# Gate projections by seven products between the steps of attention, in a one-core hybrid decoder trunk

## Chip, cores and metric

One core of one Trainium2 chip runs the whole program. The metric is the device time of one execution in microseconds (us), weights read from HBM included. All numbers are float32. The engines are TensorE (PE in the rows; PEld is its weight load), VectorE (DVE), ScalarE (ACT), GpSimd (POOL) and SyncE (SP), which issues the loads.

## What is computed

Two layers over 256 tokens of width 1024. Each layer has a mixer, a cross attention and a mixture of experts. The change lies in the mixer, of which this is the core:

```python
proj = hn @ w_in                      # columns: z, xbc, dt, q, k, v, qi, ki, wi, g_ssd, g_attn
y_ssd = ssd_branch(z, xbc, dt_raw, ...)        # scan, y * silu(z), RMSNorm in 4 groups
y_attn = dsa_branch(q, k, v, qi, ki, wi)       # top-64 keys per query, softmax, values
merged = (jax.nn.sigmoid(g_ssd) * (y_ssd @ w_ssd_o)
          + jax.nn.sigmoid(g_attn) * (y_attn @ w_attn_o))
return merged @ w_out
```

The gates g_ssd and g_attn are 1024 columns of the projection each: the products of the normalised input with two times two chunks of 512 columns.

## The kernel before

`make_order` writes out one list of stages, ORDER. Every engine goes through it and issues its own part of each stage (`stage` in each engine's block), so an engine's order is the list's order, and waits between engines are semaphores. `make_jobs` makes from ORDER the list of jobs, a job being one filling of a PSUM bank; job k uses bank (k + SHIFT) mod 8, so TensorE may fill it only when job k-8 has been read ("drained") by its owner, VectorE or ScalarE.

Weights come in chunks of 512 columns into four slots of `wring`. SP loads a chunk when the last job of the chunk four before it is filled.

Most projections use a scheme of seven products (`seven`): input and weights are cut in quarters, and seven products of quarters and of sums of quarters replace eight. PRODUCTS gives their order, 1, 2, 5, 6, 3, 7, 4. VectorE makes the sums of the input's quarters once (`sums`), four sums of weight quarters for each chunk (`weight_sums`, numbers 1 to 4), and from the seven products the four quarters of the result. ScalarE copies products 1 and 5 out of their banks (`products_1_and_5`). For the chunks of z the work is spread over the steps of the SSD scan: TensorE computes in a stage `("part", ("z", n), half)` products 1, 2, 5, 6 or 3, 7, 4, and VectorE's work on them (`join`) stands one step later. `combine` is the same work for chunks done in one piece.

The gates are done by `by_channel`: half a chunk is 16 matmuls of 256 columns, which the trace shows as 32 instructions, into two halves of a bank, and ScalarE writes their sigmoid to `gateT`.

Attention runs in six pairs of jobs. Step m of ORDER holds, in this order: the softmax division of pair m-1 (`soft`: a reciprocal and a product on VectorE), the scores of pair m (`score`: TensorE; then on VectorE the sum with the mask, the maximum and its scaling; then on ScalarE the exponentials), half a gate chunk (`part`), for m below 4 the products of y and silu(z) (`ygate`: VectorE, then squares on ScalarE), at m = 4 the normalisation of y (`ynorm`: VectorE, POOL's power, eight scalings on VectorE), the transposes of the probabilities of pair m-1 (`probT`, copied by VectorE), the product with the values of pair m-2 (`pv`, copied by ScalarE), and from m = 5 on the transposes of y (`yT`, copied by VectorE and ScalarE in turn). There are eight such steps, m = 0 to 7; steps 6 and 7 have no scores. Behind them stand `("sums", "y")` and the output projection of the SSD branch (`ssdo`), which needs all of yT.

The lines of the rows below: L785 is a matmul of `by_channel`, L816 one of `seven` with 128 columns, L819 one with 256, L742 a transpose, L960 a score, L980 a `pv`, L1475 a sum of weight quarters, L1492, L1495, L1504 and L1630 the sums of a join, L1722 to L1731 VectorE's part of an `ssd` stage, L1737 `ygate`, L1745 `ynorm`, L1760 to L1764 VectorE's part of a score, L1776 and L1778 `soft`, L1784 the copy of `probT`, L1287 a gate's sigmoid, L1347 a score's exponential, L1328 an exponential over 1024 columns in the SSD scan, L1268 a copy of yT.

## Time and profile before

| what | us |
|---|---|
| median of 3 runs | 1552.94 (1552.15 to 1553.21) |
| the profiled execution | 1552.55 |
| its span | 1550.4 |
| TensorE busy | 1407.3 |
| VectorE busy | 811.8 |
| ScalarE busy | 369.0 |

The span is what the profile covers of the execution; 2.15 us lie around it. The mean granted clock of TensorE is 0.971. Layer 0 runs to about 777 us and layer 1 from there; the attention steps lie from 234 to 313 us and from 1002 to 1081 us, the expert phases from about 555 to 777 and from about 1320 on. A row of the timeline gives the start, the time from the start of the first to the end of the last instruction, the engine, the line and how many instructions it merges; behind it, in brackets, how long the engine was idle before it and who ended that.

### The profile page before, as it was taken

Reading aid. Unit: us, or ns where it says so; the run is one execution under the profiler, and the core shown is the slowest. Engines: PE = TensorE matmul, PEld = TensorE weight load, DVE = VectorE, ACT = ScalarE, POOL = GpSimd, SP = SyncE. Lnnn points to the kernel's source line nnn. Section 1 sums busy time; section 2 is a strip of 40 time slices with the busy share of each in tenths; the row PEclk is TensorE's granted clock in tenths of the full one; section 3 lists DMA queues with packets and bytes.
Section 4 is the critical chain, followed back from the end, with each engine's and each line's share of the span. In section 5 each row is a group of like instructions: output and inputs, shape, how many; then the busy total and the mean of one; then the engine's idle time right before and its main releaser. Section 6 shows DMA issues by size and latency. Waiting matters only on the chain. (4 is left out here: it accounts for less than half of the span.)

```text
span 1550.4 us, 23297 instructions
## 1 busy us (share of the span) xinstructions
PE 1407.3 (91%) x9428; PEld 1098.2 (71%) x9428; DVE 811.8 (52%) x1562; ACT 369.0 (24%) x830; POOL 74.9 (5%) x64
## 2 busy tenths in 40 slices
PE   7999999999999978767699999999999999787684
PEld 5888888899998544334278888888999985444241
DVE  3488877577974332212135888765679643321122
ACT  2222457301111121001122234573021021110010
POOL 0000520000000000000000015100000000000000
PEclk9999999999999998899999999999999999998898
DMA  8434223246441689999963443333374408899996
GB/s 301 162 137 148 99 108 110 109 145 251 180 163 55 271 343 381 419 416 417 392 224 119 154 163 109 109 109 110 112 291 161 167 7 335 367 381 416 416 418 256
DMA packets 115706, 350.06 MB, mean 226 GB/s; under 512 B 11664, under 2 KB 13968, under 8 KB 99216
## 3 DMA queue, kind: packets, MB, share of 16 engines
q1 hardware_dynamic: 114912, 345.95, 58.1%
q0 software_dynamic: 688, 2.62, 0.4%
q8 instruction: 76, 1.25, 0.3%
q14 instruction: 30, 0.25, 0.0%
HBM read 347.50 MB, written 1.05 MB: 225 GB/s over the span
## 5 line engine op out<-in xcount | busy, mean ns | idle before, releaser
L785 PE MATMUL bank<-hT,wring 128*128 128x256 f32 x1280 | 281.9, 380 | 0.0
L785 PEld LDWEIGHTS bank<-hT,wring 128*128 128x128 f32 x1280 | 241.3, 190 | 35.9 <-issue 3.3
L1128 PE MATMUL bank<-wring,big 128*32 128x256 f32 x2048 | 140.8, 436 | 60.7 <-DMA wring<-in_w_up_e 44.4
L1128 PEld LDWEIGHTS bank<-wring,big 128*32 128x32 f32 x2048 | 70.9, 125 | 128.6 <-DMA wring<-in_w_up_e 48.2
L2033 DVE TENSOR_TENSOR h<-bank,h 128x512 f32<-128x512 f32 x64 | 44.3, 692 | 111.4 <-PE bank L1171 111.4
L2026 DVE TENSOR_TENSOR big<-bank,big 128x256 f32<-128x256 f32 x16 | 6.8, 425 | 167.4 <-ACT big L1395 167.4
L1099 PE MATMUL bank<-big,xn 128*128 128x256 f32 x256 | 74.5, 453 | 14.8 <-DVE big L1951 14.8
L1644 DVE SCALAR_TENSOR_TENSOR scr<-bank,prm,scr 128x255 f32<-128x255 f32 (+1 forms) x144 | 62.7, 477 | 47.4 <-ACT scr L1236 44.7
L1099 PEld LDWEIGHTS bank<-big,xn 128*128 128x128 f32 x256 | 67.2, 335 | 24.4 <-DVE big L1951 19.7
L816 PE MATMUL bank<-big,wring 128*128 128x128 f32 x704 | 81.3, 275 | 2.3 <-ACT big L1268 2.0
L816 PEld LDWEIGHTS bank<-big,wring 128*128 128x128 f32 x704 | 80.0, 192 | 3.0 <-issue 2.9
L1201 ACT ACTIVATE ga<-bank 128x256 f32<-128x256 f32 x48 | 18.4, 383 | 261.2 <-PE bank L816 186.1
L819 PE MATMUL bank<-wring,hT 128*128 128x256 f32 x288 | 66.1, 379 | 0.0
L819 PE MATMUL bank<-wring,xn 128*128 128x256 f32 x288 | 65.1, 379 | 0.0
L1171 PE MATMUL bank<-big 128*128 128x512 f32 x128 | 62.2, 618 | 0.1
L819 PEld LDWEIGHTS bank<-wring,xn 128*128 128x128 f32 x288 | 54.5, 190 | 10.9 <-issue 2.6
L819 PEld LDWEIGHTS bank<-wring,hT 128*128 128x128 f32 x288 | 54.4, 190 | 9.8 <-issue 2.9
L1395 ACT ACTIVATE big<-bank 128x256 f32<-128x256 f32 x16 | 6.1, 384 | 229.2 <-PE bank L1128 229.2
L766 PE MATMUL bank<-wring,qq 128*128 128x512 f32 x128 | 56.6, 595 | 0.0
L686 POOL TENSOR_TENSOR sums<-sums,cst 128x2 f32<-128x2 f32 (+2 forms) x11 | 9.0, 819 | 911.3 <-DVE sums L1428 661.2
L1475 DVE TENSOR_TENSOR wring<-wring 128x1024 f32<-128x1024 f32 (+1 forms) x36 | 51.5, 1430 | 1.2
L816 PE MATMUL bank<-hT,wring 128*128 128x128 f32 x448 | 51.7, 275 | 0.0
(320 smaller groups left out, 2228.1 us busy)
## 6 DMA issues: line engine op xcount, KB each, us to landing
wring<-in_w_in SPq DMA_DIRECT2D x68, 1024.0 KB, 7.0
wring<-in_w_gate_e SPq DMA_DIRECT2D x16, 4096.0 KB, 20.3
wring<-in_w_up_e SPq DMA_DIRECT2D x16, 4096.0 KB, 21.2
wring<-in_w_ssd_o SPq DMA_DIRECT2D x16, 1024.0 KB, 6.2
wring<-in_w_ckv SPq DMA_DIRECT2D x16, 1024.0 KB, 7.4
scr<-in_w_down_e SPq DMA_DIRECT2D x8, 2048.0 KB, 28.1
ga<-in_w_down_e SPq DMA_DIRECT2D x8, 2048.0 KB, 30.3
qq<-in_w_down_e SPq DMA_DIRECT2D x8, 2048.0 KB, 25.8
```

Of the source, the lines that this page charges most:

```text
L686: nc.gpsimd.tensor_tensor(r, r, cst[:, C_MH:C_MH + r.shape[1]], ALU.pow).then_inc(rstd_rdy, 1)
L766: ins = nc.tensor.matmul(bank[bank_of(job)][:, 0:width], src[:, k, t * P:(t + 1) * P], wring[:, SLOT[c], k, 0:width], start=i == 0, stop=i ...
L785: ins = nc.tensor.matmul(bank[bank_of(job)][:, i * SEQ:(i + 1) * SEQ], wring[:, SLOT[c], k, m:m + P], src[:, k, :], start=n == 0, stop=n = ...
L816: ins = nc.tensor.matmul(b[:, i * P:(i + 1) * P], w[:, j, i * P:(i + 1) * P], x[:, j, :], start=j == 0, stop=j == k - 1)
L819: ins = nc.tensor.matmul(b[:, 0:HALF_W], x[:, j, :], w[:, j, :], start=j == 0, stop=j == k - 1)
L1099: return nc.tensor.matmul(bank[banks[c // 2]][:, (c % 2) * E * S:(c % 2 + 1) * E * S], xn_eighth[:, k, c, :], sel[:, k, :], start=start, s ...
L1128: ins = nc.tensor.matmul(bank[b][j * S:(j + 1) * S, i * F:(i + 1) * F], xg[:, k, e:e + S], up_part[i][:, j, k * F:(k + 1) * F], start=k == ...
L1171: nc.tensor.matmul(bank[6 + n][:, :], selT[:, b, k * P:(k + 1) * P], yg[:, n * NCOL:(n + 1) * NCOL], start=True, stop=True).then_inc(sct_s, 1)
L1201: drain_inc(nc.scalar.activation(to, bank[bank_of(JOB[(st, p)])][:, 0:HALF_W], ACT.Copy), JOB[(st, p)])
L1475: V.tensor_tensor(out, a, b, ALU.subtract).then_inc(wsum_rdy, 1)
L1644: ins = V.scalar_tensor_tensor(conv[:, m % 2, i, k:SEQ], b[:, i * SEQ:(i + 1) * SEQ - k], prm[:, w:w + 1], conv[:, m % 2, i, k:SEQ], ALU.m ...
L2033: V.tensor_tensor(hh, bank[6 + n][:, :], hh, ALU.add).then_inc(add_s, 1)
```

## The change

It does five things in each layer:

- the four gate chunks are made by seven products, four of them in the first half and three in the second; their joins stand a step later, between `soft` and `score`;
- the chunks come in the order attention gate, then SSD gate (`GATES`);
- the sigmoid is taken of a whole gate at a time, in `gateT` in place: of the attention gate in step 5, ahead of score 5, of the SSD gate behind the last join;
- the copies of `probT` and all copies of yT go to ScalarE, and the eight scalings of `ynorm` too;
- the router's weights, whose place in `btok` now holds temporaries of the joins, are loaded later.

```diff
@@ -80,6 +80,9 @@
 PAIRS = [(t, i) for t in range(2) for i in range(2 * (t + 1))]
 ATT = [(t, r, i) for t, i in PAIRS for r in range(2)]
 SSD = [(t, g) for t in range(TT) for g in range(SG)]
+
+
+GATES = [("gate", 1, 0), ("gate", 1, 1), ("gate", 0, 0), ("gate", 0, 1)]
 
 
 def make_order():
@@ -102,9 +105,13 @@
     for m in range(len(PAIRS) + 2):
         if 1 <= m <= len(PAIRS):
             o += [("soft", 2 * m - 2), ("soft", 2 * m - 1)]
+        if m:
+            o += [("join", GATES[(m - 1) // 2], (m - 1) % 2)]
+        if m == 5:
+            o += [("sigmoid", 1)]
         if m < len(PAIRS):
             o += [("score", m)]
-        o += [("part", ("gate", m // 4, m // 2 % 2), m % 2)]
+        o += [("part", GATES[m // 2], m % 2)]
         if m < 4:
             o += [("ygate", 2 * m), ("ygate", 2 * m + 1)]
         if m == 4:
@@ -115,6 +122,7 @@
             o += [("pv", m - 2)]
         if m >= 5:
             o += [("yT", i) for i in ((0, 1), (2, 3, 4), (5, 6, 7))[m - 5]]
+    o += [("join", GATES[3], 1), ("sigmoid", 0)]
     o += [("sums", "y"), ("ssdo", 0), ("ssdo", 1), ("sums", "att"), ("atto", 0), ("mem",), ("atto", 1), ("sums", "merged")]
     o += [("memT", i) for i in range(4)] + [("sums", "mem"), ("wo", 0), ("wo", 1)]
     o += [("norm", 1), ("ck", 0)] + [("hT", 1, i) for i in range(4)] + [("ck", 1), ("sums", "h")]
@@ -145,8 +153,8 @@
     "hT": (1, "both"), "small": (2, "dve"), "kv": (2, "dve"), "qi": (2, "dve"), "xbc": (2, "dve"),
     "acum": (1, "dve"), "kT": (1, "dve"), "kiT": (1, "dve"), "qiT": (1, "act"), "idx": (2, "act"),
     "xT": (1, "act"), "bT": (1, "act"), "cb": (1, "dve"), "qT": (1, "act"), "decay": (2, "act"),
-    "score": (2, "dve"), "probT": (1, "dve"), "pv": (1, "act"), "gate": (2, "act"),
-    "yT": (1, "both"), "memT": (1, "act"),
+    "score": (2, "dve"), "probT": (1, "act"), "pv": (1, "act"),
+    "yT": (1, "act"), "memT": (1, "act"),
     "xscore": (1, "act"), "xprobT": (1, "act"), "xpv": (1, "dve"), "co": (2, "dve"),
     "hX": (1, "act"), "router": (1, "dve"), "rank": (1, "dve"), "count": (1, "dve"),
 }
@@ -158,10 +166,10 @@
     return ["dve", "act" if SSD[n][0] == 0 else "dve"]
 
 
-SEVEN = {"q": "h0", "z": "h0", "ssdo": "y", "atto": "att", "wo": "merged", "ck": "mem", "cv": "mem", "cq": "h"}
+SEVEN = {"q": "h0", "z": "h0", "gate": "h0", "ssdo": "y", "atto": "att", "wo": "merged", "ck": "mem", "cv": "mem", "cq": "h"}
 PRODUCTS = (1, 2, 5, 6, 3, 7, 4)
 HALVES = (PRODUCTS[:4], PRODUCTS[4:])
-EARLY = ("q", "z")
+EARLY = ("q", "z", "gate")
 UNITS = [st[1] if st[0] == "part" else st for st in ORDER
          if st[0] in SEVEN or st[0] == "part" and st[1][0] in SEVEN and st[2] == 0]
 FIRST_OF = {"h0": (("q", 0), (1, 2)), "y": (("ssdo", 0), (1, 2, 3))}
@@ -377,6 +385,7 @@
         *late_temps, whole0, whole1 = [cols(att, i * HALF_W, HALF_W) for i in range(7)]
         wholes = [whole0, whole1]
         early_temps = [cols(mix, 1792 + i * HALF_W, HALF_W) for i in range(3)] + [cols(att, 1536 + i * HALF_W, HALF_W) for i in range(2)]
+        gate_temps = early_temps[:3] + [cols(btok, i * HALF_W, HALF_W) for i in range(2)]
         sums_of = {"h0": xn[:, :, :].rearrange("p t (s k n) -> p (t s) k n", s=2, n=P),
                    "y": [cols(big, 4096 + i * 1024, KC, P) for i in range(2)]
                    + [cols(hT[:, :, :].rearrange("p c t -> p (c t)"), i * 1024, KC, P) for i in range(2)],
@@ -404,10 +413,14 @@
 
         def temps(st):
 
+            if st[0] == "gate":
+                return gate_temps
             return early_temps if st[0] in EARLY else late_temps
 
         def spare_sums(st):
 
+            if st[0:2] == ("gate", 0):
+                return cols(scr, 2048, KC // 2, HALF_W), cols(scr, 3072, KC // 2, HALF_W)
             if st[0] in EARLY:
                 return cols(ga, 0, KC // 2, HALF_W), cols(ga, 1024, KC // 2, HALF_W)
             if st[0] == "ssdo":
@@ -477,6 +490,7 @@
         wsum_rdy = sem("sums_of_weight_quarters")
         q_rdy = sem("queries_roped")
         z_rdy = sem("z_silu_ready")
+        g_rdy = sem("gate_sigmoid_ready")
         mem_sq = sem("mem_squares")
         mem_eps = sem("mem_mean_square")
         mem_rstd = sem("mem_rstd_ready")
@@ -652,9 +666,9 @@
                         settle(sp)
                         src = w_down[l, 1, 0:BE].rearrange("j (k p) n -> p k j n", p=P)
                         sp.dma_start(mix_rows, src[:, 0]).then_inc(mix_in, 16)
-                    if c == CHUNK[(("ssdo", 1), 1)]:
-
-                        filled(sp, l, JOB[(("ssd", SG - 1), 1)])
+                    if c == CHUNK[(("cq", 0), 0)]:
+
+                        drained(sp, l, JOB[(GATES[3], 4)])
                         settle(sp)
                         sp.dma_start(rw[:, :, 0:G], rows(w_group[l], 0, G)).then_inc(router_in, 16)
                         sp.dma_start(rw[:, :, G:G + G * E], rows(w_router[l], 0, G * E)).then_inc(router_in, 16)
@@ -833,14 +847,12 @@
                 elif kind in ("small", "kv", "qi"):
                     by_token(l, st, hT, {"small": SH + HD + IH, "kv": 2 * AKV * HD}.get(kind, NCOL),
                              blocks_by={k: JOB[(("hT", 0, k // 2), 0)] for k in range(KC)} if kind == "small" else None)
-                elif kind == "part" and st[1][0] == "gate":
-                    by_channel(l, st[1], hT, tiles=st[2:3])
                 elif kind == "part" and st[1][0] == "co":
                     by_token(l, st[1], qT, tile_by=CO_TILE_BY, tiles=st[2:3], ks=range(KC // 2 if st[2] else 0, KC))
                 elif kind == "open":
                     by_token(l, st[1], qT, tile_by=CO_TILE_BY, tiles=st[2:3], ks=range(KC // 2))
                 elif kind == "part":
-                    seven(l, st[1], {}, products=HALVES[st[2]])
+                    seven(l, st[1], {}, by_channel=st[1][0] == "gate", products=HALVES[st[2]])
                 elif kind == "q":
                     seven(l, st, {})
                 elif kind == "xbc":
@@ -1279,13 +1291,28 @@
                         if n >= 2:
                             act.wait_ge(rel_used, l * 2 * len(IDX) + (n - 1))
                         drain_inc(nc.scalar.activation(rel[:, n % 2, :], bank[bank_of(job)][:, :], ACT.Relu), job)
-                elif kind == "part" and st[1][0] == "gate":
-                    _, st, j = st
-                    job = JOB[(st, j)]
+                elif kind == "sigmoid":
+
+                    g = st[1]
+                    drained(act, l, JOB[(("gate", g, 1), 4)])
+                    for i in range(2):
+                        rows = gateT[g][:, 4 * i:4 * i + 4, :].rearrange("p c t -> p (c t)")
+                        ins = nc.scalar.activation(rows, rows, ACT.Sigmoid)
+                    ins.then_inc(g_rdy, 1)
+                elif kind == "ynorm":
+
+                    act.wait_ge(rstd_rdy, l * NORMS + 2)
+                    for t in range(TT):
+                        for g in range(SG):
+                            y = xs[:, t, g * NCOL:(g + 1) * NCOL]
+                            ins = nc.scalar.activation(y, y, ACT.Copy, scale=st_[:, 8 + t * SG + g:9 + t * SG + g])
+                    ins.then_inc(yn_rdy, 1)
+                elif kind == "probT":
+                    n = st[1]
                     filled(act, l, job)
-                    blk = 4 * st[2] + 2 * j
-                    drain_inc(nc.scalar.activation(gateT[st[1]][:, blk:blk + 2, :].rearrange("p c t -> p (c t)"),
-                                                   bank[bank_of(job)][:, :], ACT.Sigmoid), job)
+                    if n >= 4:
+                        filled(act, l, JOB[(("pv", (n - 4) // 2), 0)])
+                    drain_inc(nc.scalar.activation(pT[:, n % 4, :], bank[bank_of(job)][:, :], ACT.Copy), job)
                 elif kind == "part" and st[1][0] in SEVEN:
                     if st[2] == 0:
                         products_1_and_5(l, st[1])
@@ -1626,6 +1653,10 @@
 
                     def put(a, b, x, y, op):
 
+                        if of[0] == "gate":
+                            blk = 4 * of[2] + 2 * b
+                            dst = gateT[of[1]][:, blk:blk + 2, a * P:(a + 1) * P]
+                            return V.tensor_tensor(dst, x.rearrange("p (c t) -> p c t", t=P), y.rearrange("p (c t) -> p c t", t=P), op)
                         n = of[1] * NCOL + b * HALF_W
                         return V.tensor_tensor(zt[:, a, n:n + HALF_W], x, y, op)
 
@@ -1738,12 +1769,7 @@
                 elif kind == "ynorm":
 
                     dve.wait_ge(ssq_rdy, (l + 1) * len(SSD))
-                    rms(l * NORMS + 2, st_[:, 0:8], st_[:, 8:16], NCOL)
-                    for t in range(TT):
-                        for g in range(SG):
-                            y = xs[:, t, g * NCOL:(g + 1) * NCOL]
-                            ins = V.tensor_scalar(y, y, st_[:, 8 + t * SG + g:9 + t * SG + g], None, ALU.mult)
-                    ins.then_inc(yn_rdy, 1)
+                    V.tensor_scalar(st_[:, 8:16], st_[:, 0:8], 1.0 / NCOL, EPS, ALU.mult, ALU.add).then_inc(var_rdy, 1)
                 elif kind == "score":
                     for r in range(2):
                         n = 2 * st[1] + r
@@ -1776,12 +1802,6 @@
                     link(V.reciprocal(rs[:, n % 4, 0:nh], sm[:, n % 4, 0:nh]))
                     s3 = sco[:, n % 4, :].rearrange("p (h s) -> p h s", h=nh)
                     V.tensor_tensor(s3, s3, bc(rs[:, n % 4, 0:nh], 2, NCOL // nh), ALU.mult).then_inc(pr_rdy, 1)
-                elif kind == "probT":
-                    n = st[1]
-                    filled(dve, l, job)
-                    if n >= 4:
-                        filled(dve, l, JOB[(("pv", (n - 4) // 2), 0)])
-                    drain_inc(V.tensor_copy(pT[:, n % 4, :], b), job)
                 elif kind == "xpv":
                     t, pr = divmod(st[1], 2)
                     filled(dve, l, job)
@@ -1794,7 +1814,7 @@
 
                         blk = 4 * st[1] + 2 * b
                         rows, ts = slice(blk, blk + 2), slice(a * P, (a + 1) * P)
-                        drained(dve, l, JOB[(("gate", g, st[1]), b)])
+                        dve.wait_ge(g_rdy, l * 2 + 2 - g)
                         whole = wholes[(a + b) % 2]
                         link(V.tensor_tensor(whole, x, y, op))
                         of = whole.rearrange("p (c t) -> p c t", t=P)
```

What moves is told by the order of the built programs. The first place is VectorE in an odd and an even step (rows print the line of their own kernel; `bank` is PSUM, `scr` at that place is `gateT`, `ga` holds scores, `mix` and `btok` the temporaries). Before, from the gatings of y in step 3 to the scores of step 4:

```order
L1737 TENSOR_TENSOR xs<-xs,big 128x512 [waits z_silu_ready] x2
L1784 COPY qq<-bank 128x512 [waits bank_filled] x2
L1776 RECIPROCAL rs<-sm 128x2 [waits score_exp_ready]
L1778 TENSOR_TENSOR ga<-ga,rs 128x512 [waits dve_step]
L1776 RECIPROCAL rs<-sm 128x2 [waits score_exp_ready]
L1778 TENSOR_TENSOR ga<-ga,rs 128x512 [waits dve_step]
L1760 TENSOR_TENSOR ga<-bank,mix 128x512 [waits bank_filled]
```

With the change:

```order
L1768 TENSOR_TENSOR xs<-xs,big 128x512 [waits z_silu_ready] x2
L1802 RECIPROCAL rs<-sm 128x2 [waits score_exp_ready]
L1804 TENSOR_TENSOR ga<-ga,rs 128x512 [waits dve_step]
L1802 RECIPROCAL rs<-sm 128x2 [waits score_exp_ready]
L1804 TENSOR_TENSOR ga<-ga,rs 128x512 [waits dve_step]
L1659 TENSOR_TENSOR scr<-bank,btok 128x2x128 [waits bank_filled]
L1502 TENSOR_TENSOR scr<-wring 128x1024 [waits bank_filled,chunk_in2]
L1502 TENSOR_TENSOR scr<-wring,scr 128x1024 [waits bank_filled,sums_of_weight_quarters]
L1531 TENSOR_TENSOR btok<-bank,mix 128x256 [waits bank_filled]
L1659 TENSOR_TENSOR scr<-btok,mix 128x2x128 [waits drained_by_dve]
L1659 TENSOR_TENSOR scr<-btok,bank 128x2x128 [waits bank_filled,dve_step]
L1786 TENSOR_TENSOR ga<-bank,mix 128x512 [waits bank_filled]
```

The copies of `probT` have gone, and six sums, two of them over 1024 columns, stand between the divisions and the next score. The second place is ScalarE behind the exponentials of step 4. Before:

```order
L1287 ACT_TABLE_LOAD
L1287 ACTIVATE scr<-bank 128x512 [waits bank_filled]
L1368 ACTIVATE qq<-bank 128x2x128 [waits bank_filled]
L1347 ACT_TABLE_LOAD
L1347 ACTIVATE ga,sm<-ga,nmx 128x256 [waits score_max_ready]
```

With the change:

```order
L1213 ACTIVATE mix<-bank 128x256 [waits drained_by_dve,bank_filled] x2
L1308 ACTIVATE xs<-xs,sums 128x512 [waits rstd_ready]
L1308 ACTIVATE xs<-xs,sums 128x512 x7
L1315 ACTIVATE qq<-bank 128x512 [waits bank_filled] x2
L1395 ACTIVATE qq<-bank 128x2x128 [waits bank_filled]
L1300 ACT_TABLE_LOAD
L1300 ACTIVATE scr<-scr 128x1024 [waits drained_by_dve]
L1300 ACTIVATE scr<-scr 128x1024
L1374 ACT_TABLE_LOAD
L1374 ACTIVATE ga,sm<-ga,nmx 128x256 [waits score_max_ready]
```

The scalings of y, the copies of `probT` and the sigmoid of a whole gate now stand between the exponentials of step 4 and those of step 5; in the other steps the pairs of table loads are gone.

## Rows read from the trace of the kernel before

**Rows 1.** Busy time by stretch: layer 0's attention, one step of it, the expert phase.

```profile
core 0: us, PE busy (x) PEld busy (x) DVE busy (x) ACT busy (x) POOL busy (x), PEclk, DMA share, GB/s
234.02:313.26 79.24, 78.22 (x442) 64.05 (x441) 47.56 (x100) 45.82 (x114) 1.65 (x1) 1.00 0.30 110
251.29:261.34 10.05, 10.05 (x53) 7.82 (x53) 7.97 (x17) 7.55 (x19) 0.00 (x0) 1.00 0.59 210
560.00:790.00 230.00, 170.47 (x1458) 89.61 (x1448) 45.10 (x100) 29.31 (x57) 0.70 (x1) 0.91 0.98 397
```

**Rows 2.** Timeline of TensorE, one step of attention in layer 1.

```profile
1030.27 7.17 PE L785 MATMUL bank<-hT,wring 128*128 128x256 f32 x32
1037.28 1.04 PE L742 MATMUL bank<-cst,ga 128*128 128x128 f32 x8
1038.25 1.08 PE L980 MATMUL bank<-qq,mix 128*64 128x512 f32 x4
1039.26 1.13 PE L960 MATMUL bank<-mix,qq 64*128 64x256 f32 x8
```

**Rows 3.** Timeline of TensorE, products of the SSD output projection, layer 1.

```profile
1088.35 7.31 PE L816 MATMUL bank<-big,xs 128*128 128x128 f32 x64
1095.50 7.31 PE L816 MATMUL bank<-hT,wring 128*128 128x128 f32 x64
```

**Rows 4.** Timeline of VectorE, soft and score of step 5, layer 1.

```profile
1050.29 0.15 DVE L1776 RECIPROCAL rs<-sm 128x2 f32<-128x2 f32 x1
...
1051.89 0.68 DVE L1760 TENSOR_TENSOR ga<-bank,mix 128x512 f32<-128x512 f32 x1
...
1053.53 0.69 DVE L1760 TENSOR_TENSOR ga<-bank,mix 128x512 f32<-128x512 f32 x1
```

**Rows 5.** Groups by line and shape, VectorE, 234 to 313 us.

```profile
L1784 DVE COPY qq<-bank 128x512 f32<-128x512 f32 x12 | 7.7, 686 | 15.4 <-PE bank L742 15.4
...
L1737 DVE TENSOR_TENSOR xs<-xs,big 128x512 f32<-128x512 f32 x8 | 5.1, 684 | 0.0
```

**Rows 6.** Timeline of VectorE, the scalings of y, layer 0.

```profile
278.05 3.26 DVE L1745 TENSOR_SCALAR xs<-xs,sums 128x512 f32<-128x512 f32 x8 [1.76 <-POOL sums L686]
```

**Rows 7.** Timeline of VectorE, joins of z, layer 0.

```profile
210.72 0.41 DVE L1630 TENSOR_TENSOR big<-bank,ga 128x256 f32<-128x256 f32 x1
...
214.96 0.69 DVE L1722 TENSOR_TENSOR xs<-bank,xs 128x512 f32<-128x512 f32 x1 [0.19 <-PE bank L935]
...
219.42 1.21 DVE L1475 TENSOR_TENSOR wring<-wring 128x1024 f32<-128x1024 f32 x1
220.56 0.41 DVE L1630 TENSOR_TENSOR big<-bank,mix 128x256 f32<-128x256 f32 x1
...
230.62 0.42 DVE L1630 TENSOR_TENSOR big<-bank,ga 128x256 f32<-128x256 f32 x1
```

**Rows 8.** Timeline of ScalarE, second score of step 2, layer 0.

```profile
257.19 0.51 ACT L1347 ACTIVATE ga<-ga,nmx 128x256 f32<-128x256 f32 x1 [0.55 <-DVE nmx L1764]
...
258.30 1.28 ACT L1287 ACT_TABLE_LOAD   x1
259.59 0.60 ACT L1287 ACTIVATE ga<-bank 128x512 f32<-128x512 f32 x1
```

**Rows 9.** Groups by line and shape, ScalarE, whole program.

```profile
L1328 ACT ACTIVATE scr<-scr 128x1024 f32<-128x1024 f32 x16 | 16.9, 1057 | 0.4
```

**Rows 10.** Timeline of ScalarE, a copy of yT, layer 0.

```profile
302.45 0.84 ACT L1268 ACTIVATE big<-bank,prm 128x256 f32<-128x256 f32 x2 [0.63 <-PE bank L742]
```

**Rows 11.** Queue of SP around the loads of router weights and of w_cq, layer 0.

```profile
311.38 2.87 SPq L660 DMA_DIRECT2D btok<-in_w_router  x1
...
427.04 15.17 SPq L593 DMA_DIRECT2D wring<-in_w_cq  x4
```

**Rows 12.** Start of layer 1: busy time by stretch, and TensorE's timeline.

```profile
775.00:780.00 5.00, 2.66 (x13) 2.69 (x14) 1.80 (x4) 1.77 (x3) 0.70 (x1) 0.72 1.05 390
...
777.34 3.50 PE L742 MATMUL bank<-cst,xn 128*128 128x128 f32 x16 [5.30 <-ACT xn L1211]
```

## The prediction

> **What bounds the kernel now.** I read four views, from coarse to fine. Busy time by stretch comes first. In the expert phase TensorE has 0.74 of the time and the DMA engines 0.98 [rows 1]: weights arrive as fast as they can, so that phase neither hides a change ahead of it nor gives time back; it starts later or earlier by as much as the phase before it ends. In the attention steps TensorE is busy for the whole of a step (10.05 of 10.05 us), VectorE for 7.97 and ScalarE for 7.55, at a granted clock of 1.00 [rows 1]. The timeline of such a step says what the 10.05 us are: 7.01 for half a gate chunk, 0.97 for the eight transposes of probabilities, 1.01 for the product with the values, and the rest, 1.06, for the scores [rows 2]. So TensorE's own work is the bound in all eight steps, and VectorE sits beside it with about 2 us to spare in a step. The stretch from the first score (234.02 us) to the first product of the SSD output projection (313.26) lasts 79.2 us [rows 1] and stands in both layers.
>
> **The change, part by part, for one layer.** A step m runs from score m to score m+1. I hand results from VectorE or ScalarE on with 0.2 us (the waits of 0.19 in [rows 7] are of that size) and from TensorE with 0.33, a choice with which the same laying-out gives back the measured stretch.
>
> *TensorE, removed and added.* Eight half chunks of 7.01 us go: 56.1. A product of two quarters is 16 instructions with 128 columns; four such products start 7.15 us apart [rows 3]. Four half chunks of four products (7.15) and four of three (5.36) are 50.0 us. If nothing else moved, a layer would gain 6.1 us.
>
> *VectorE, removed.* Twelve copies of transposed probabilities, 0.686 us each, 8.2 in all, and four pairs of scalings of yT [rows 5]; and the eight scalings of y, 3.26, with the wait for POOL's power ahead of them, 1.76 [rows 6]. All of it lay in VectorE's spare time.
>
> *VectorE, added.* The first half of a join is two sums of weights and three of products: 1.14 (start to start) + 1.22 + three sums at 0.41, with their hand-overs 1.28, = 3.64 us. The second half, with the first two weight sums of the next chunk in it, is 4.05 (4.24 between its start and the next operation's, of which 0.19 is that one's own wait) [rows 7]. These are joins of z; those of the gates have the same shapes. The join of z that stands last before attention starts at 230.62 and gets two weight sums more; at 4.06 it ends at 234.7. The three operations of the last SSD part, 0.69 each and 2.35 with hand-overs, follow, and the first score's own work begins at 237.0. What stays on VectorE: two softmax divisions 1.62, two scores 2 x 1.64 = 3.28 [rows 4], in steps 0 to 3 two gatings of y 1.26 (0.68 each, 0.63 start to start) [rows 5].
>
> *The steps, VectorE against TensorE.* VectorE needs 1.62 + 3.64 + 3.28 + 1.26 = 9.80 us for an odd step and 1.62 + 4.05 + 3.28 + 1.26 = 10.2 for an even one; TensorE needs 1.06 + 5.36 + 0.97 + 1.01 = 8.40 and 1.06 + 7.15 + 0.97 + 1.01 = 10.19. A pair is 20.0 us on VectorE and 18.6 on TensorE; before, it was 20.1. TensorE can't run ahead, since a product's bank comes free only with the join of the step before, and that join stands behind the softmax of its own step. So VectorE becomes the bound up to step 4, and the saving is eaten there. I laid the steps one behind the other from 237.0: VectorE ends its scores of steps 1 to 4 at 251.4, 261.6, 271.4 and 280.6. In an even step TensorE gets its first bank only at the join's first operation and its second 2.8 us later, behind the two weight sums; so it finishes step 4 at 283.8 (now 281.4) though it has less to do.
>
> *ScalarE, steps 4 and 5.* Here is the one long wait that I expect. ScalarE has finished the exponentials of step 4 at 281.7, copies two products (0.76), scales y eight times at 0.52 (4.2; nearest row: a copy of 512 columns, 0.60 long and 0.49 to the next), copies two probT and one pv (1.4): 288.2. Then it loads the sigmoid's table, 1.28, runs two sigmoids over 1024 columns, near 2.1 by an exponential of that size, loads the exponential's table, 1.28 [rows 8, 9], and only then, at 292.8, takes the exponentials of step 5, whose maxima were ready at 289.7. They take 1.1 a score, the first ends at 293.9, both divisions at 296.0; VectorE was idle for 4.4 us. Its first sum of the next join then frees the bank for gate part 6. TensorE, done with step 5 at 293.1, starts it at 296.5, its second product at 299.3, behind two weight sums, and has finished the part at 304.7.
>
> *The end.* From there TensorE is the bound again: transposes, pv and three yT 3.3, gate part 7 5.4, pv 1.0; the first of the last three yT is filled at 314.9. All three are now copied by ScalarE, 0.84 each [rows 10], behind a pv copy: 317.8. The SSD projection starts at 317.95. The same laying-out with the kernel before gives 313.40 for a measured 313.26, so the method is good to some tenths there. The difference is 4.6 us a layer. Behind it the last sigmoid (1.28 + 2.1) lies beside the projection's first 7 us and is hidden; without that cover it would cost 3.4. The loads of router weights (issue 2.87 us) go from behind the last load of w_ssd_o to between two loads of w_cq, whose four issues now span 15.17 us [rows 11]: they fill a gap of SP's queue and cost nothing; without the gap up to 2.9 us.
>
> *Table loads.* In the trace a load takes 1.28 us and the next ACTIVATE begins right behind it (258.30, 259.59 [rows 8]). The twelve loads in a layer's steps lay beside TensorE's work and their going gains nothing; two of the four left lie on the path above, at 1.28. The Trainium skill, page "ScalarE: Activation LUTs", section "What ACT_TABLE_LOAD costs", has some 1283 ns for the load and 1380 ns of drain with it for each switch. By that page the detour would be 2.8 us longer a layer and the time some 1567 us; the row shows no such drain, and the sum goes by the row.
>
> **The sum.** 2 x 4.6 = 9.2 us on the profiled execution's 1552.55: 1561.8, so 1562. The median of the runs, 1552.94, is 0.4 above that execution, which I leave in the rounding. Bounds: if only TensorE's work counted, 1552.6 - 12.2 = 1540.3; if hand-overs between engines cost 0.4 instead of 0.2, the same laying-out gives 6.0 us a layer, 1564.6.
>
> **Rivals.**
> *Faster: TensorE stays the bound.* The mechanism is bank reuse that costs nothing, because joins find their place while TensorE works. For it: VectorE is busy for 47.6 us of the stretch now [rows 1]; less 8.2, 3.3 and 3.5 for what goes (four pairs of yT at 0.84 to 0.88), and with 28.4 for the joins (4 x 3.64 + 3 x 4.05 + 1.66 for the last, which has no weight sums), that is some 61 us of the 73 that TensorE would need. Against it: each even step asks 10.2 us of VectorE in a fixed order. It decides if softmax and join of one step take under 8.4 us with the scores. Time: 1540.3. Chance 0.06.
> *No change: the detour of ScalarE is hidden.* If the exponentials of step 5 don't wait for the sigmoid and the two loads, VectorE's 4.4 us go, step 6 starts 4 us earlier, and 0.6 us a layer is left: 1553.7. Against it: the sigmoid of the first gate stands ahead of score 5 on ScalarE in the order shown. Chance 0.10.
> *Slower still: the clock falls.* TensorE would wait 3.4 us before gate part 6. Behind a wait of 5.30 us at a layer's start the granted clock was 0.72 over 5 us, which mixes 1.2 and 2.4 GHz, and 16 transposes took 3.50 us, where eight take 0.97 [rows 12, 2]. So a fall would cost near 1.6 us a layer: 1565. The Trainium skill, page "TensorE: Matmul & The Clock Gate", part 1, says that an idle array goes to 1.2 GHz and that activity gives 2.4 back; the fall in this row agrees; whether a wait of 3.4 us brings it, no row here shows. Chance 0.12, as the other waits before this point are under 2 us.
> *The forecast itself.* Chance 0.72, by itself 1557 to 1565.
>
> **Numbers.** 0.2% is 3.1 us, about what a measurement of this kernel can tell from no change. Slower by more than that: the forecast but for a small part, and the clock: 0.82. Within: 0.11. Faster: 0.07. The range goes from 1553, which takes in the hidden detour, to 1567, with the clock's fall and slower hand-overs; outside are the rival of 1540 and the tails, under 2 in 10.
>
> **What would show it.** Right: the first product of the SSD projection starts 4 to 5 us later than now from the layer's first score on, in both layers; waits of TensorE on VectorE near 1 to 2 us in steps 2 to 4 and one of 3 us or more at gate part 6; VectorE idle some 4 us for ScalarE's exponentials in step 5, behind two table loads and eight scalings; the stretches after it as long as before. Wrong: steps 1 to 4 shorter than 10 us on the mean, or VectorE waiting for banks that TensorE fills, or a difference that appears outside the two stretches of attention.

## The result, and the profile after

The changed kernel takes 1561.12 us (median of 6 runs, 1560.21 to 1563.34), the kernel before 1553.53 (6 runs, 1552.15 to 1554.97): ratio 1.0052, 95% interval 1.0042 to 1.0062. That is 7.6 us slower, against 9.2 in the forecast, and 0.9 below the forecast time of 1562.0. The profiled execution took 1560.21 us and its span is 1558.4, 8.0 above the span before.

Where the time went is read first from one window, from the first score to the first product of the SSD output projection (columns as in [rows 1]):

```profile
core 0: us, PE busy (x) PEld busy (x) DVE busy (x) ACT busy (x) POOL busy (x), PEclk, DMA share, GB/s
234.27:317.88 83.61, 75.73 (x634) 67.95 (x633) 61.97 (x117) 48.85 (x138) 1.65 (x1) 0.98 0.30 108
```

The stretch lasts 83.61 us and lasted 79.24 [rows 1]. TensorE is busy for 2.5 us less in it, VectorE for 14.4 more, ScalarE for 3.0 more, and the granted clock is no longer 1.00. In layer 1 it is 83.60 for 79.24. Behind it little moved: from the projection's first product to the first matmul whose operands are `wring` and `big`, in this order, with 256 columns, 127.79 us passed in layer 0 before and after. Further on, the router of layer 0 took 0.36 us longer, since TensorE waited 1.17 us for VectorE there and not 0.81; in layer 1 it did not. Why stays open.

Timeline of TensorE, changed kernel, layer 0: the scores of steps 2, 3 and 5, and every row of the stretch in which TensorE waited for another engine.

```profile
250.23 1.13 PE L972 MATMUL bank<-mix,qq 64*128 64x256 f32 x8
...
256.13 3.84 PE L830 MATMUL bank<-xn,ga 128*128 128x128 f32 x32 [0.67 <-DVE btok L1531]
...
261.80 1.13 PE L972 MATMUL bank<-mix,qq 64*128 64x256 f32 x8
264.58 3.84 PE L830 MATMUL bank<-xn,wring 128*128 128x128 f32 x32 [1.65 <-DVE scr L1659]
...
275.76 2.05 PE L830 MATMUL bank<-hT,wring 128*128 128x128 f32 x16 [0.61 <-DVE btok L1531]
...
283.20 1.13 PE L972 MATMUL bank<-mix,qq 64*128 64x256 f32 x8
...
296.07 5.44 PE L830 MATMUL bank<-hT,wring 128*128 128x128 f32 x32 [3.27 <-DVE ga L1659]
301.35 3.74 PE L830 MATMUL bank<-xn,scr 128*128 128x128 f32 x32
...
317.88 2.36 PE L830 MATMUL bank<-big,wring 128*128 128x128 f32 x19 [1.61 <-ACT big L1280]
```

Three waits on VectorE's joins in steps 2 to 4 (0.67, 1.65, 0.61) take the place of TensorE's solid steps [rows 2]; the score of step 5, at 281.45 before, starts at 283.20. Then comes the long one, 3.27 us, before gate part 6, and the first two products of that part need 5.28 us (296.07 to 301.35) where the next two need 3.57. The 1.61 at the end, for the last copy of yT, was 1.02 before.

That VectorE sets the pace up to step 4 is seen in its own busy time, the fourth column:

```profile
237.00:280.00 43.00, 40.00 (x338) 35.89 (x337) 40.55 (x79) 22.35 (x82) 0.00 (x0) 1.00 0.30 113
```

It is busy for 40.55 of 43.00 us, and its timeline shows no wait for another engine from 229.73 to 281.05; what is missing lies in the short hand-overs between its own operations.

Behind the long wait stands ScalarE. Its timeline, from the last exponential of step 4 to the first of step 5:

```profile
280.43 0.49 ACT L1374 ACTIVATE ga<-ga,nmx 128x256 f32<-128x256 f32 x1
280.83 0.19 ACT L1374 ACTIVATION_READ_ACCUMULATOR ga<-ga,nmx 128x1 f32 x1
280.92 0.63 ACT L1213 ACTIVATE mix<-bank 128x256 f32<-128x256 f32 x2
281.73 5.01 ACT L1308 ACTIVATE xs<-xs,sums 128x512 f32<-128x512 f32 x8 [0.17 <-POOL sums L700]
286.64 1.06 ACT L1315 ACTIVATE qq<-bank 128x512 f32<-128x512 f32 x2
287.60 0.37 ACT L1395 ACTIVATE qq<-bank 128x256 f32<-128x256 f32 x1
287.98 1.28 ACT L1300 ACT_TABLE_LOAD   x1
289.28 2.00 ACT L1300 ACTIVATE scr<-scr 128x1024 f32<-128x1024 f32 x2
291.30 1.28 ACT L1374 ACT_TABLE_LOAD   x1
292.60 0.51 ACT L1374 ACTIVATE ga<-ga,nmx 128x256 f32<-128x256 f32 x1
```

And VectorE, which has the maxima ready and waits for these exponentials before the divisions and the next join:

```profile
279.72 0.17 DVE L1790 TENSOR_SCALAR nmx<-mx 128x2 f32<-128x2 f32 x1
...
288.57 0.17 DVE L1790 TENSOR_SCALAR nmx<-mx 128x2 f32<-128x2 f32 x1
293.72 0.17 DVE L1802 RECIPROCAL rs<-sm 128x2 f32<-128x2 f32 x1 [4.98 <-ACT ga L1374]
...
295.51 0.42 DVE L1659 TENSOR_TENSOR ga<-bank,btok 128x256 f32<-128x256 f32 x1
```

The row at 295.51 is the join's first sum: it frees the bank for which TensorE waits until 296.07. What TensorE's clock did there is in windows of 2 us:

```profile
294.00:296.00 2.00, 0.00 (x0) 0.00 (x0) 1.88 (x5) 2.00 (x8) 0.00 (x0) 1.00 1.03 396
296.00:298.00 2.00, 1.93 (x12) 1.96 (x13) 1.97 (x2) 1.36 (x4) 0.00 (x0) 0.70 0.52 193
298.00:300.00 2.00, 2.00 (x11) 2.00 (x11) 1.93 (x5) 0.38 (x1) 0.00 (x0) 0.50 0.02 4
300.00:302.00 2.00, 2.00 (x19) 2.00 (x18) 1.13 (x2) 0.00 (x0) 0.00 (x0) 0.95 0.00 0
```

A granted clock of 0.50 is the lower level, 1.2 GHz: after the wait TensorE ran at half speed for most of two products.

### The profile page after: what moved, and what is told of

It reads as the page before. It is cut to its first block, busy times and chain, and to the rows that moved or that the text cites. A ratio compares the mean times of both kernels' runs of the same rounds, so it can differ in the third digit from the quotient of the medians.

```text
span 1558.4 us, 24237 instructions
## 1 busy us (share of the span) xinstructions
PE 1402.7 (90%) x9812; PEld 1106.3 (71%) x9812; DVE 842.4 (54%) x1594; ACT 378.0 (24%) x878; POOL 74.9 (5%) x64
## 4 chain that ended last, share of the span: by engine, by line
PE 66%; issue 16%; DMA 8%; DVE 6%; ACT 3%; SPq 0%; DVEq 0%; POOL 0%; POOLq 0%; ACTq 0%
PE bank L830 19%; PE bank L833 15%; PE bank L799 11%; PE bank L780 7%; DMA ga<-in_w_down_e 6%; PE bank L756 3%; PE bank L1111 2%; PE bank L1140 2%; PE bank L947 1%; DMA wring<-in_w_up_e 1%; PE bank L1183 1%; PE bank L1036 1%; PE bank L936 1%; DVE ga L1502 1%; PE bank L1166 1%
## 5 line engine op out<-in xcount | busy, mean ns | idle before, releaser
L799 PE MATMUL bank<-hT,wring 128*128 128x256 f32 x768 | 167.5, 380 | 0.0
L830 PE MATMUL bank<-hT,wring 128*128 128x128 f32 x832 | 102.2, 282 | 7.9 <-DVE ga L1659 6.5
L1502 DVE TENSOR_TENSOR wring<-wring 128x1024 f32<-128x1024 f32 (+1 forms) x44 | 61.2, 1392 | 1.2
```

The lines of the kernel that those rows point to most:

```text
L799: ins = nc.tensor.matmul(bank[bank_of(job)][:, i * SEQ:(i + 1) * SEQ], wring[:, SLOT[c], k, m:m + P], src[:, k, :], start=n == 0, stop=n = ...
L830: ins = nc.tensor.matmul(b[:, i * P:(i + 1) * P], w[:, j, i * P:(i + 1) * P], x[:, j, :], start=j == 0, stop=j == k - 1)
L1502: V.tensor_tensor(out, a, b, ALU.subtract).then_inc(wsum_rdy, 1)
```

## The experiments

The theory: up to step 5 VectorE sets the pace, because the joins and the sums of weights are on it; from step 5 on it is ScalarE's detour (scalings, table load, sigmoid, table load) and the clock behind the wait that it makes. Rivals: the moves to ScalarE are the cause by themselves; table loads drain the engine and cost more than their rows; the clock's fall has nothing to do with the wait.

Single profiled executions of these kernels differ by up to 3 us outside attention, on the way through the router and the experts of a layer. The stretch of attention does not: before, changed and the experiments repeat it between the layers to 0.02 us, but for two runs named below. So I judge by the stretch, split at the score of step 5, as read from TensorE's timeline (layer 0):

| kernel | score 0 to score 5 | score 5 to SSD projection | stretch | time, us |
|---|---|---|---|---|
| before | 47.43 | 31.81 | 79.24 | 1553.53 |
| changed | 48.93 | 34.68 | 83.61 | 1561.12 |
| e1 sigmoid at end | 48.93 | 29.54 | 78.47 | 1553.02 |
| e2 and sums behind join | 48.05 | 29.61 | 77.66 | 1551.20 |
| e3 more work on VectorE | 53.25 | 35.85 | 89.10 | 1572.45 |
| e4 narrow sums | 45.04 | 31.21 | 76.25 | 1546.62 |
| e5 scalings on VectorE | 48.93 | 36.23 | 85.16 | 1564.43 |
| e6 and sigmoid at end | 48.92 | 36.19 | 85.11 | 1564.05 |
| e7 moves alone | 47.42 | 32.40 | 79.82 | 1553.68 |
| e8 TensorE kept busy | 48.93 | 33.93 | 82.86 | 1560.86 |
| e9 Exp for Sigmoid | 48.94 | 31.07 | 80.01 | not readable |
| e10 e4 and e1 together | 45.04 | 29.54 | 74.58 | 1545.56 |

**e1: the sigmoid of step 5 goes behind the last join.**

```diff
-        if m == 5:
-            o += [("sigmoid", 1)]
...
-    o += [("join", GATES[3], 1), ("sigmoid", 0)]
+    o += [("join", GATES[3], 1), ("sigmoid", 1), ("sigmoid", 0)]
```

> The sigmoid of the attention gate goes from ahead of score 5 to behind the last join, beside the other one. Theory (ScalarE's detour holds the chain in step 5): VectorE no longer waits 5 us for the exponentials of step 5, TensorE's wait of 3.3 us before gate part 6 goes, and with it the fall of the clock; the stretch from the first score to the first product of the SSD projection goes from 83.6 to about 79.1 us in each layer, the time from 1561.1 to about 1552. Rival (VectorE's load alone is the cause): the wait moves elsewhere and the time stays within 1.5 us of 1561.

Measured: 1553.02 us (11 runs), ratio 0.9996, interval 0.9987 to 1.0005; stretch 78.47. All of the change's loss is gone, and in the stretch 0.8 us a layer besides. The time doesn't show that 0.8: the kernel before took 1553.44 us (21 runs) beside these runs. Timeline of TensorE at gate part 6, where the wait of 3.27 stood:

```profile
292.60 1.10 PE L754 MATMUL bank<-cst,xs 128*128 128x128 f32 x8
293.53 3.74 PE L828 MATMUL bank<-hT,wring 128*128 128x128 f32 x32
```

No wait, and two products in 3.6 us. The first five steps are the same to 0.01 us, so the sigmoid's place acts on what follows step 5 alone: 5.14 us. ScalarE still scales y for 5 us there; it is the first load, the sigmoids and the second load on top of that which made it late.

**e2: as e1, and the gates' first two sums of weights of the next chunk at the end of the join instead of in its middle.**

```diff
-                if after[0] in EARLY:
+                if after[0] in ("q", "z"):
                     weight_sums(l, after, (1, 2))
...
                 drain_inc(put(1, 0, part3, b, ALU.subtract), job)
+                if after[0] == "gate":
+                    weight_sums(l, after, (1, 2))
```

> As e1, and the first two weight sums of the next gate chunk stand at the end of a join's second half, no longer between its first and second operation, so that the banks of products 3, 7 and 4 come free earlier. Theory (in even steps TensorE waits for banks, 0.6 to 0.7 us each before product 2): stretch about 78.1 us, time about 1550, which is below the kernel before. Rival: product 5 then waits for the sums instead by as much, and the time equals that of e1.

Measured: 1551.20 us (11 runs), ratio 0.9988, interval 0.9979 to 0.9997; stretch 77.66. The banks come free before the 2.4 us of sums of weights instead of after them, and the first five steps are 0.9 us shorter. This is the one version that leaves nothing out and whose interval lies below the kernel before, by 0.12%, near the limit of what the runs can tell.

**e3: twelve reductions over 512 columns more on VectorE in each layer, one with each probT.**

```diff
+                elif kind == "probT":
+                    link(V.tensor_reduce(top8[:, 0:1], cst[:, 0:NCOL], AX_X, ALU.max))
```

> VectorE gets back, as a plain maximum over 512 columns of constants whose result nobody uses, the twelve operations of 0.69 us a layer that the change took from it (the copies themselves stay on ScalarE). Theory (VectorE is the bound of steps 1 to 4): about 3.7 to 5.5 us a layer longer, 1569 to 1572. Rival (VectorE has slack in these steps, the loss is all in step 5): within 1.5 us of 1561.

Measured: one execution, 1572.45 us; stretch 89.10, so of the 8.4 us added (1.40 a pair) 5.5 appear. Three of the six pairs stand ahead of the join of step 4, and that join and score 5 come 4.32 us later, which is all that these pairs take: VectorE has no slack there. Of the later pairs 2.3 us go into its wait for the exponentials, which falls from 4.98 to 2.70. The other 1.2 us of loss, behind score 5, match a longer fall of the clock. Two rows behind waits are

```profile
267.23 5.47 PE L830 MATMUL bank<-xn,wring 128*128 128x128 f32 x32 [3.09 <-DVE scr L1659]
...
300.16 6.62 PE L830 MATMUL bank<-hT,wring 128*128 128x128 f32 x32 [3.01 <-DVE ga L1659]
```

against 3.84 and 3.74 for such rows at full clock. From the start of the second row to that of the next product it is 6.46 us, for 5.28 in the changed kernel. The slow row at 267.23 costs nothing, for VectorE does not wait for its products.

**e4: the gates' sums of weights cut to one column (which leaves these sums out).**

```diff
+                    if st[0] == "gate":
+                        out, a, b = [v[:, 0:1, 0:1] for v in (out, a, b)]
                     V.tensor_tensor(out, a, b, ALU.subtract).then_inc(wsum_rdy, 1)
```

> The sixteen sums of weight quarters for the gates in each layer are cut to one column each; they signal as before. It leaves out nearly all of these sums, so the gates are not what they should be. Theory (VectorE's joins hold the bank reuse): steps 1 to 4 become TensorE's 8.4 to 10.2 us and the stretch goes to about 76 us in each layer, the time to about 1546, with the wait for ScalarE in step 5 still there. Rival (products wait for something else): over 1557.

Measured: one execution, 1546.62 us; stretch 76.25. The first five steps take 45.04 us for 48.93: 3.9 us a layer are what VectorE's sums of weights put on the path before score 5. VectorE's wait for the exponentials of step 5 is still there:

```profile
DVE rs L1804 <- ACT ga L1374: 4.4, 2, 4.2
```

That row of the waits (total, times, longest) has 4.2 us for the longest.

**e5 and e6: the eight scalings of y back on VectorE; e5 with the sigmoid in its place, e6 with both sigmoids at the end.**

```diff
-                            ins = nc.scalar.activation(y, y, ACT.Copy, scale=st_[:, 8 + t * SG + g:9 + t * SG + g])
...
+                            ins = V.tensor_scalar(y, y, st_[:, 8 + t * SG + g:9 + t * SG + g], None, ALU.mult)
```

> The changed kernel with the eight scalings of y back on VectorE, sigmoid in its place. Theory (the sigmoids hold the exponentials of step 5, and VectorE is short of time by about as much): VectorE gets 8 x 0.40 = 3.2 us more work in step 4 while ScalarE gets 5.0 us less; the exponentials come earlier, VectorE comes later, so nearly nothing is gained: stretch 83.3 us (changed kernel 83.6), time about 1560.5, and the wait of VectorE for the exponentials shrinks from 5.0 to under 2 us. Rival (the scalings in ScalarE's queue are the cause by themselves): 5.0 us of ScalarE's path go, up to the whole loss comes back: stretch about 79, time about 1552.

> The same with both sigmoids behind the last join, as in e1 (stretch 78.5 there, scalings on ScalarE). Theory: with the detour gone VectorE is what bounds, so its 3.2 us of scalings come onto the path and more by the hand-overs behind them: stretch 83.3 us, time about 1561, 4.8 us a layer over e1. Rival (ScalarE is the scarce engine, VectorE hides the scalings in its waits): as e1 or below it, 78.5 us, time 1553.

Measured, one execution each: 1564.43 and 1564.05 us, both slower than the changed kernel and than either expectation; stretches 85.16 and 85.11 in layer 0, but 83.71 and 83.64 in layer 1. The rivals fall: the scalings on ScalarE are not the cause, and taking them back is worth less than nothing. With them on VectorE the sigmoid's place changes nothing, since VectorE is the later of the two (its longest wait for exponentials is 0.4 us in both, for 4.98); with them on ScalarE it changes 5.1. The two layers of e5 differ at one place, gate part 5 (first row layer 0, second layer 1):

```profile
288.63 6.70 PE L830 MATMUL bank<-xn,wring 128*128 128x128 f32 x32 [3.76 <-DVE ga L1651]
...
1063.05 5.26 PE L830 MATMUL bank<-xn,wring 128*128 128x128 f32 x32 [3.77 <-DVE ga L1651]
```

The same wait, and 1.44 us between the rows, as between the stretches (1.45). The granted clock was 0.58 over the 8 us from 288 and 0.74 over the 6 us from 1063:

```profile
288.00:296.00 8.00, 7.37 (x40) 7.38 (x41) 7.13 (x16) 3.03 (x9) 0.00 (x0) 0.58 0.01 3
...
1063.00:1069.00 6.00, 5.95 (x40) 5.95 (x41) 5.54 (x11) 2.01 (x8) 0.00 (x0) 0.74 0.00 0
```

Against a row of 3.84 at full clock the fall cost 2.9 us in one layer and 1.4 in the other, and without it both stretches would be 82.3. My expectation of 83.3 had no term for a fall there. What made it longer in layer 0 stays open.

**e7: the kernel before with only the moves to ScalarE (copies of probT and yT, scalings of y).**

```diff
-    "score": (2, "dve"), "probT": (1, "dve"), "pv": (1, "act"), "gate": (2, "act"),
-    "yT": (1, "both"), "memT": (1, "act"),
+    "score": (2, "dve"), "probT": (1, "act"), "pv": (1, "act"), "gate": (2, "act"),
+    "yT": (1, "act"), "memT": (1, "act"),
...
```

The part left out moves the code of these copies and scalings to ScalarE, as in the change.

> The kernel before (gates as plain products, a sigmoid with each copy) with only the change's moves to ScalarE: copies of probT and of yT, scalings of y. Theory: TensorE bounds the steps there at 10.05 us and nothing else is late, so VectorE's relief is worth nothing until the tail, where the last three copies of yT stand on one engine instead of two: stretch 79.2 + 0.6 = 79.8 us, time about 1554.7 (ratio 1.0008). Rival (the moves by themselves cost what the change lost): 83.6 us, 1562. Rival (they gain, and the seven products cost more than was measured): below 78.5 us, under 1552.

Measured: 1553.68 us (10 runs), ratio 1.0004, interval 0.9994 to 1.0013; stretch 79.82, so 0.58 a layer, all of it behind score 5. The moves neither cost what the change lost nor gain.

**e8: the second yT job's four transposes issued seven times over, so that TensorE works through most of the wait.**

```diff
-                    ins = nc.tensor.transpose(b[:, i * P:(i + 1) * P], src, ident)
+                    ins = nc.tensor.transpose(b[:, i % 4 * P:(i % 4 + 1) * P], src, ident)
...
-                    transposes(l, JOB[(st, 0)], pairs(xs, st[1]))
+                    transposes(l, JOB[(st, 0)], pairs(xs, st[1]) * (7 if st[1] == 1 else 1))
```

> The changed kernel with the four transposes of the second yT job issued seven times over (28 in place of 4), so that TensorE is busy through most of the 3.3 us in which it waited at 293 to 296 us. Same results. Theory (the granted clock fell to 0.50 to 0.70 at 296 to 300 us because TensorE had stood still before): clock 1.00 there, first two products of part 6 take 3.6 us and not 5.3, but the second waits for its bank until 298.9, so the stretch is shorter by about 0.7 us a layer: 82.9 us, time about 1559.8. Rival (the fall has nothing to do with the wait): clock 0.5 to 0.7 in the same place, stretch 83.6 or longer, time 1561 or above.

Measured: 1560.86 us (4 runs; ratio to the kernel before 1.0053, interval 1.0037 to 1.0070); stretch 82.86. Timeline of TensorE and its clock at the place of the fall:

```profile
291.77 3.71 PE L756 MATMUL bank<-cst,xs 128*128 128x128 f32 x32
296.14 2.02 PE L830 MATMUL bank<-hT,wring 128*128 128x128 f32 x16 [0.66 <-DVE ga L1659]
298.78 2.05 PE L830 MATMUL bank<-hT,wring 128*128 128x128 f32 x16 [0.61 <-DVE btok L1531]
300.66 3.74 PE L830 MATMUL bank<-xn,scr 128*128 128x128 f32 x32
```

```profile
296.00:298.00 2.00, 1.86 (x16) 1.86 (x16) 1.97 (x2) 1.42 (x4) 0.00 (x0) 1.00 0.59 218
298.00:300.00 2.00, 1.39 (x13) 1.23 (x12) 1.93 (x5) 0.38 (x1) 0.00 (x0) 1.00 0.05 12
```

With work in place of the wait the clock stayed at 1.00, part 6 started no earlier, and its first two products took 4.52 us instead of 5.28: the fall cost 0.76. At full clock the wait for the second bank, 0.61, shows, which the slow product had covered. The time itself can't resolve 1.5 us; the rows do.

**e9: Exp in place of the sigmoid of step 5 (the gate of attention gets other values).**

```diff
-                        ins = nc.scalar.activation(rows, rows, ACT.Sigmoid)
+                        ins = nc.scalar.activation(rows, rows, ACT.Exp if g else ACT.Sigmoid)
```

> The changed kernel with Exp in place of the sigmoid of step 5 (the gate of attention gets other values), so that no table load stands between the exponentials of steps 4 and 5. Theory (a table load costs its 1.28 us and nothing behind it): ScalarE's queue loses 2 x 1.28 us, the exponentials of step 5 come 2.56 us earlier, TensorE's wait of 3.3 us shrinks to about 0.7 us and the clock stays at 1.00: stretch 83.6 - 2.6 = 81.0 us, down to 80.7, time about 1556. Rival (ScalarE drains for another 1.38 us at each load, as the Trainium skill, ScalarE: Activation LUTs, 'What ACT_TABLE_LOAD costs', has it): up to 5.3 us a layer, stretch 78.3, time about 1551. Rival (the loads lie beside other work): 83.6, 1561.

Measured: stretch 80.01, 3.60 less than the changed kernel, against 2.6 to 2.9 expected. The time of its one execution, 1614.3 us, is not comparable: with other values the tokens are routed otherwise, and the experts' weights are loaded 18 times instead of 16 (first row e9, second the changed kernel, DMA issues of the page):

```profile
wring<-in_w_gate_e SPq DMA_DIRECT2D x18, 4096.0 KB, 20.2
```

```profile
wring<-in_w_gate_e SPq DMA_DIRECT2D x16, 4096.0 KB, 20.2
```

ScalarE's timeline without the loads:

```profile
288.15 2.00 ACT L1300 ACTIVATE scr<-scr 128x1024 f32<-128x1024 f32 x2
290.04 0.51 ACT L1374 ACTIVATE ga<-ga,nmx 128x256 f32<-128x256 f32 x1
```

From the first score the exponentials of step 5 start at 55.48 us instead of 58.33: two loads cost 2.85 us, 1.42 each, that is 1.28 and some 0.14 for two ACTIVATEs that otherwise overlap a little. The other 0.75 is the clock, which stayed up: part 6's first two products took 4.53 us.

**e10: e4 and e1 together; leaves the gates' sums of weights out.**

> e1 (both sigmoids behind the last join) with e4's gates' sums of weights cut to one column; leaves these sums out. It frees both things that the theory holds to be in the way: ScalarE's detour and VectorE's 4.7 us of weight sums per gate half. Theory: what is left is TensorE's saving of 6.1 us a layer less 0.6 to 0.9 for the last copies of yT and the hand-overs: stretch 79.2 - 5.2 = 74.1 us, time 1543. Rival (something else holds the steps, banks or hand-overs between engines): no more than e4's 76.2 us, time 1546 or above.

Measured: one execution, 1545.56 us, 2.6 above the expectation, of which layer 0 lost 2.1 between the first matmul on `wring` and `big` and its last expert's up projection (317.0 us for 314.9 before); 1.9 of that lie in the router, where the clock fell (last section). The stretch is 74.58, 4.66 below the kernel before. Its two parts are those of e4 (45.04) and of e1 (29.54), so the two causes act one after the other. Timeline of TensorE, gate parts 0 and 1, nothing waits in them:

```profile
235.35 3.84 PE L828 MATMUL bank<-hT,wring 128*128 128x128 f32 x32
239.03 3.74 PE L828 MATMUL bank<-xn,ga 128*128 128x128 f32 x32
242.70 1.16 PE L970 MATMUL bank<-mix,qq 64*128 64x128 f32 x16
243.79 3.84 PE L828 MATMUL bank<-xn,wring 128*128 128x128 f32 x32
247.46 1.95 PE L828 MATMUL bank<-hT,wring 128*128 128x128 f32 x16
249.25 1.04 PE L754 MATMUL bank<-cst,ga 128*128 128x128 f32 x8
```

Four products take 7.35 us here and three 5.46. Over the eight parts it is 7.35 + 7.25 + 7.25 + 7.14 + 4 x 5.46 = 50.8 us; the saving is 56.1 - 50.8 = 5.3, and less 0.58 for the tail (e7) that is the 4.66.

**The ledger of a layer.** Before 79.24. TensorE's products less, and the last copies of yT on one engine (e7, +0.58): together -4.66, e10. VectorE's sums of weights: +3.89 (e10 to e1), all before score 5. The sigmoid and its tables between the exponentials: +5.14 (e1 to changed), all behind it; 2.85 of that are the two loads and 0.76 the clock (e9, e8). The rest, 1.5, goes to the sigmoids' own 2.0 us: e9 keeps operations of that length in the place, e1 has none there, and its stretch is 1.54 shorter. Sum: 83.61. These sizes hold in this order: without the sums of weights the detour costs 1.67 only (e10 to e4).

## Why the prediction was right

- **The sum.** 4.6 us a layer forecast, 4.37 and 4.36 measured. The medians differ by 7.6 us, the two profiled spans by 8.0 and two stretches by 8.7. Of the 0.7 between the last two, 0.54 lie in layer 1 behind the projection, where the kernel before took 128.34 us and the changed one 127.80; the rest is within the spread of the runs (3.1 us for the changed kernel).
- **TensorE's saving was mis-sized.** "Four half chunks of four products (7.15) and four of three (5.36) are 50.0 us" took its pace from the SSD projection. In the gates they take 50.8 (e10): 5.3 us saved a layer, not 6.1. So with the tail's 0.58 the faster rival could have given no less than 1543, not 1540.3.
- **VectorE as the bound up to step 4: right.** Its scores of step 4 ended at 279.9 (forecast 280.6), and TensorE's step 4 at 283.2 (283.8); steps 1 to 4 took 10.12 us on the mean. TensorE's single waits were mostly smaller than the 1 to 2 us forecast (0.67, 1.65, 0.61). e3 and e4 show the bound from both sides: more work on VectorE appears in the time, less gives 3.9 us back.
- **ScalarE's detour: right, its parts nearly.** Exponentials of step 5 at 292.60 (292.8), VectorE idle 4.98 (4.4), part 6 at 296.07 (296.5), projection at 317.88 (317.95). The scalings were mis-sized, 5.0 us for 4.2: the nearest row was a copy out of a bank, and two of these start 0.48 us apart (286.64 to 287.60), while the eight scalings start 0.61 apart (281.73 to 286.64). The scalings read from SBUF and take a scale for each partition; no run tells which of the two costs more. e5 shows that ScalarE was still the better place for them.
- **The clock: a rival's mechanism came with the forecast's.** It had a chance of 0.12 and a price of 1.6 us a layer. It fell in both layers, and the slow products lost 1.7 us (5.28 for 3.57), but 0.95 of it lay over the wait for the second bank, which the sum had in the same place. The net price is 0.76 (e8). Without the fall a layer would have lost 3.62 us (e8), so the laying-out itself was 1.0 too high: in e8 part 6 starts 61.81 us behind the first score, 0.7 earlier than forecast, and the way from its end to the projection takes 12.95 us (304.24 to 317.19) for 13.25. Two errors of opposite sign made 4.37 look like 4.6; that closeness is luck. The Trainium skill, "TensorE: Matmul & The Clock Gate", part 1, has an idle array at 1.2 GHz and activity bring 2.4 back; the changed kernel and e8 agree with that.
- **Table loads: the row was the better price.** In the changed kernel the next ACTIVATE begins 0.02 us behind the load's end (291.30 + 1.28, 292.60), and e9 measures 1.42 us for a load with all it brings. The Trainium skill, "ScalarE: Activation LUTs", "What ACT_TABLE_LOAD costs", adds 1380 ns of drain to each switch; by an estimate from that page (two switches) e9 would have saved 5.3 us where it saved 2.85, and the measurement decides.
- **The tail, the last sigmoid, the router's loads: right.** 0.58 for 0.6 by e7; the last sigmoid's load starts at 317.75 beside the projection, and the 127.79 us behind the stretch are the same to 0.01 us in layer 0. The loads of router weights show no price.
- **The rival "no change"** (1553.7) is nearly what e1 measures, when one entry of the order is moved: 1553.0. The detour was worth 5.1 us a layer there, where the rival gave it 4.

That the copies of probT or yT could have stayed on VectorE was not tried: banks are drained in the order of their jobs on each engine, and with joins one step later this order would not hold. Sums of weights on another engine than VectorE were not tried either.

## What to carry to other kernels

A saving on the engine that bounds is worth what the engine beside it can keep up with: lay out its new work step by step in its fixed order, and price the pace of the saved work in its own surroundings. Put work that switches ScalarE's table where no exponential is queued behind it; here the same sigmoid cost 5.1 us a layer in one place and nothing that shows in another. A wait of TensorE is paid twice when the clock falls behind it, less whatever wait the slow matmuls then cover.

## What the runs showed of the hardware

- The granted clock fell to the lower level behind waits of 3.01, 3.09, 3.27 and 3.76 us (e3, changed, e5), and not behind the waits of 1.65 and 1.61 us in the changed kernel. In the changed kernel it was still 1.00 in the last 2 us of the wait and 0.50 over 298 to 300, while matmuls ran again.
- The length of the wait alone does not decide it. In the router of layer 0 TensorE waited 1.17 us in e1, in e10 and in the changed kernel alike. In e1 and e10 the clock fell behind that, and the twenty matmuls there took 6.60 us; in the changed kernel it stayed at 1.00, and they took 5.12. In e1:

```profile
549.58 0.41 PE L1091 MATMUL bank<-rt,cst 128*128 128x32 f32 x2 [1.17 <-DVE rt L1944]
...
550.05 6.60 PE L1109 MATMUL bank<-big,xn 128*128 128x256 f32 x20
...
552.00:554.00 2.00, 2.00 (x7) 1.55 (x6) 0.88 (x2) 1.51 (x2) 0.00 (x0) 0.50 0.97 401
```

In the changed kernel:

```profile
554.30 5.12 PE L1111 MATMUL bank<-big,xn 128*128 128x256 f32 x20
```

- The same wait, in the same kernel, was followed by falls that cost 2.9 us in one layer and 1.4 in the other (e5; e6 nearly the same).
- Two ACT_TABLE_LOADs cost 2.85 us in ScalarE's queue (e9), 1.28 each by their rows.
- The stretch of attention repeated between layers to 0.02 us in ten of twelve kernels, while the way from the first matmul on `wring` and `big` to the last expert's up projection in layer 0 ranged from 314.6 to 317.4 us over kernels that have the same work there. A place in the timeline tells tenths of a microsecond that the whole time can't.
